# Time mix's preparation with two k units among the low-rank products, and r's mixture on ScalarE and GpSimd

## The chip, the cores and the metric

The kernel runs on one core of a Trainium2 chip. The metric is the device time of one launch in microseconds, the median of several runs; before the change it is 2626.39 us in 3 runs (2619.64 to 2627.75).

## What is computed

The program is a whole two-part network on 272 rows (16 meta rows and 256 inputs) of 1024 features: a first part with attention, a gated layer, a *time mix* and a layer of 8 experts, and a second part of two blocks. The change lies in the time mix alone. Cut to what matters here:

```python
dx_prev, dx_next = shift(x, 1) - x, shift(x, -1) - x
xs = x[None] + mu[0] * dx_prev + mu[1] * dx_next          # six mixtures
r, k, v = xs[0] @ w_r, xs[1] @ w_k, xs[2] @ w_v
lw[n] = tanh(xs[3] @ w1[n]) @ w2[n]                       # n: the two directions
decay = exp(-exp(-softplus(-(w0 + lw)) - 0.5))
a[n]  = sigmoid(a0 + (xs[4] @ a1[n]) @ a2[n])
g  = sigmoid(xs[5] @ g1) @ g2
kk = k * k_k;  kk = kk / max(norm_by_head(kk), 1e-12)
kd[n] = k * (1 + (a[n] - 1) * k_a)
y = scan(r, decay[0], kd[0], v, kk, a[0]) + reverse_scan(r, decay[1], kd[1], v, kk, a[1])
```

Behind it stand a norm by head, a bonus, the gate g, the output product and a layer norm.

## The kernel before, in words

Every engine has a program of its own, written out by hand: TensorE (PE), VectorE (DVE), ScalarE (ACT), GpSimd (POOL) and SyncE (SP). Each engine runs its instructions strictly in that order, and they meet through counting semaphores: `pe.at("k_sq", f)` is the point at which ACT has finished the square of tile f. Nothing is planned at run time, so an instruction that waits holds up all that stands behind it on its engine.

Activations lie with 128 features on partitions and the 272 rows along the free axis, so a tensor is 8 tiles of 128x272, called f or k = 0..7. A *unit* is one output tile: 8 matmuls of 128x272 that sum over k (`unsplit_units`, L358; the trace shows each of these float32 matmuls as two records, so x16 for a unit).

The time mix runs, on PE: eight units of v (L358), the first halves of the two low-rank chains (`lora_in`, L1015), their second halves (`lora_out`, L1026, 32 products), eight units of k (L358) with, two units behind each, a head sum of the squares of kk (L1044), the gate's hidden layer in 128 and in 32 columns (L1054), the spread of the reciprocal norm over the heads (L999, 8 tiles of two products), and eight units of r (L358), into which the first products of the scan are set: `first` (L1079) behind r 3 and the transposes `forward` (L1091) behind r 5. Then comes the scan over ten groups (5 chunks in 2 directions), in three waves of 4, 4 and 2 groups (`pre` L1148/L1157, `back` L1102/L1112, levels L1120, `res` L1171/L1172, `upd` L1181, `y` L1194 to L1196, `grown` L1206/L1207).

Beside it DVE makes the mixtures: `mix(i, k)` is two instructions (L1413, L1415) with a wait between, in the order i = 2 (v), 3, 4 (low rank), 1 (k), 5 (gate), 0 (r), eight tiles each. Then it scans the decays (L1438) and subtracts (L1440), scales k (L1444), makes the rate (L1462) and half of k's tensors (`half_k(d, f)` L1451/L1453, four tiles at a time), takes the norm (L1466), its reciprocal (L1468), clears buffers (L1470 to L1477), multiplies kk with the spread norm (L1481), makes BE and KE (L1484, L1486), and the solves of the waves (L1503 to L1531). ACT copies finished units out of PSUM (L1270), applies the low-rank nonlinearities (L1276, L1282, 32 sigmoids), the exponentials (L1288 to L1292), the squares for the head sums (L1299), k's factor (L1310), the square root of the norm (L1313) and the gate's sigmoid (L1316). POOL does nothing in the time mix until the bonus.

PSUM has eight banks, and every user takes one by a counter that turns unless it names a bank itself; it waits for whoever held that bank before:

```python
def bank(event, *key, b=None):
    if b is None:
        b = turn[0] % 8
        turn[0] += 1
    before, holder[b] = holder.get(b), (event, *key)
```

`forward` and `back` always take banks 4 to 7 by name. So who waits for whom in the scan hangs on how often the counter was turned before it. In the kernel before, r 0 gets bank 7, r 6 bank 1 (held by r 2), `upd` 0 bank 5 and `y` 0 bank 7, both last held by the second wave's `forward`.

Of the kernel before, what the change touches and what calls it, by code (L numbers as in the profile page):

```python
# [9 lines left out]
ACT = mybir.ActivationFunctionType  # L10
# [4 lines left out]
KC = 8  # L15
# [5 lines left out]
CH = 55  # L21
# [22 lines left out]
for _n, _w in PARAMS:  # L44
# [20 lines left out]
    "rw_out": "rv k r decays exp prep rate_taken k_part less_ka bonus bonus.kd",  # L65
# [100 lines left out]
def build(nc, A, out, known=None, stages=99):  # L166
# [774 lines left out]
    def by_chunk(x):  # L941
        return x[:, :, 0:NCH * CH].rearrange("p f (c t) -> p f c t", t=CH)
# [49 lines left out]
    def rwkv_pe(pe):  # L992
# [25 lines left out]
        def lora_out(key, x):  # L1018
# [3 lines left out]
            for f in range(KC):  # L1022
                for n in range(2):
                    b, before = bank("lora", key, f, n)
                    pe.wait_ge(pe.at(*before))
                    t = e.matmul(PS[:, b, 0:T], w2v[64 * n:64 * n + 64, f * 128:(f + 1) * 128], x[64 * n:64 * n + 64, :],  # L1026
                                 start=True, stop=True)
                    t.then_inc(*pe.sig("lora_mm", key, f, n))
            pe.also("direct", "A", m)
# [19 lines left out]
        for j, w in enumerate([128, 32]):  # L1049
            b, before = bank("gate_h", j)  # L1050
            pe.wait_ge(pe.at(*before))
            for k in range(KC):
                pe.wait_ge(pe.at("mixed", 5, k))
                t = e.matmul(PS[0:w, b, 0:T], gv[:, k, j * 128:j * 128 + w], MIXED[5][:, k, :], start=k == 0, stop=k == KC - 1)  # L1054
            t.then_inc(*pe.sig("gate_h_mm", j))
        pe.also("direct", "A", m)
        pe.wait_ge(pe.at("k_norm_r"))
        for f in range(KC):
            b, before = bank("k_spread", f)
            pe.wait_ge(pe.at(*before))  # L1060
            spread(b, f).then_inc(*pe.sig("k_spread_mm", f))
# [203 lines left out]
    def rwkv_act(act):  # L1265
# [19 lines left out]
        def exps(d):  # L1285
# [3 lines left out]
            e.activation(fac[d], by_chunk(rw_s[d])[:, :, :, CH - 1], ACT.Exp, scale=-KAPPA).then_inc(*act.own())  # L1289
            act.wait_ge(act.last)  # L1290
            e.activation(KE[d], KE[d], ACT.Exp, scale=sign).then_inc(*act.sig("exp", d, "ke"))
            e.activation(RE[d], RE[d], ACT.Exp, scale=sign).then_inc(*act.sig("exp", d, "re"))  # L1292

# [10 lines left out]
        for d in range(2):  # L1304
            exps(d)
            for f in range(4 * d, 4 * d + 4):
                k_square(f)
            act.wait_ge(act.at("rate_taken", d))
            for f in range(KC):
                e.activation(rw_a[d][:, f, 0:T], rw_a[d][:, f, 0:T], ACT.Identity, bias=less_ka[:, f:f + 1],  # L1310
                             scale=par("k_a", f)).then_inc(*act.sig("k_part", d, f))
# [96 lines left out]
    def rwkv_dve(dve):  # L1408
# [8 lines left out]
        for k in range(0, KC, 2):  # L1417
# [4 lines left out]
            e.tensor_copy(rw_e[:, r, T:T + 1], H[:, r, T - 1:T]).then_inc(*dve.own())  # L1422
# [6 lines left out]
        for i in (3, 4, 1, 5, 0):  # L1429
            for k in range(KC):  # L1430
                mix(i, k)

        def decays(d):
            dve.wait_ge(dve.at("lora", "w_lora", 7, 1))
            dve.wait_ge(dve.at("c_rw"))
            dve.wait_ge(dve.last)
            for f in range(KC):
                e.tensor_tensor_scan(rw_s[d][:, f, :], cst[:, 0:TS], rw_c[d][:, f, :], 0.0, MUL, ADD).then_inc(*dve.own())  # L1438
            dve.wait_ge(dve.last)
            e.tensor_tensor(rw_c[d], rw_s[d], rw_c[d], SUB).then_inc(*dve.sig("decays", d))  # L1440

# [45 lines left out]
        for d in range(2):  # L1487
            half_k(d, 4)
# [1856 lines left out]
```

## Time and profile before

| | |
|---|---|
| median of 3 runs | 2626.39 us (2619.64 to 2627.75) |
| profiled execution, its own time | 2621.39 us |
| its span | 2619.5 us |
| mean granted clock of TensorE | 0.981 |
| time mix, up to the scan | about 406 to 530 us |
| scan | about 530 to 750 us |

The profile is a page of one execution (busy time of every engine, the share of it in 40 slices, the chain of waits, the costliest groups), and behind it the trace, which answers by instruction: a timeline of one engine in a stretch, its waits by releaser, the busy time of all engines in a stretch. In a timeline row the first number is the start from the beginning of the span, the second the busy time of the group, then the engine, line, operation, output and inputs, the count, and in brackets how long the engine was idle before and what released it.

### The profile page before, as it was taken

Reading aid. Unit: us, or ns where it says so; the run is one execution under the profiler, and the core shown is the slowest. Engines: PE = TensorE matmul, PEld = TensorE weight load, DVE = VectorE, ACT = ScalarE, POOL = GpSimd, SP = SyncE. Lnnn points to the kernel's source line nnn. Section 1 sums busy time; section 2 is a strip of 40 time slices with the busy share of each in tenths; the row PEclk is TensorE's granted clock in tenths of the full one; section 3 lists DMA queues with packets and bytes.
Section 4 is the critical chain, followed back from the end, with each engine's and each line's share of the span. In section 5 each row is a group of like instructions: output and inputs, shape, how many; then the busy total and the mean of one; then the engine's idle time right before and its main releaser. Section 6 shows DMA issues by size and latency. Waiting matters only on the chain. (4 is left out here: it accounts for less than half of the span.)

```text
span 2619.5 us, 47732 instructions
## 1 busy us (share of the span) xinstructions
PE 2518.9 (96%) x20277; PEld 2083.1 (80%) x20277; DVE 1974.1 (75%) x2831; ACT 1531.2 (58%) x2229; POOL 176.8 (7%) x192
## 2 busy tenths in 40 slices
PE   8999999999998999999999999999999999999998
PEld 7779997688976667676676767666897999998998
DVE  7855538654446999898999999988686885677874
ACT  5634423522223778787887878786546664537653
POOL 0000000020002260000000000010010201010201
PEclk9989999999999999999999999999999999999999
DMA  7325543230032899999999999997454645444742
GB/s 203 105 65 162 177 161 87 91 103 4 4 112 82 322 383 370 377 373 377 371 370 379 369 374 375 375 367 297 122 165 128 193 153 172 148 138 145 207 137 97
DMA packets 264613, 565.86 MB, mean 216 GB/s; under 512 B 25996, under 2 KB 204356, under 8 KB 221260
## 3 DMA queue, kind: packets, MB, share of 16 engines
q1 hardware_dynamic: 257580, 547.02, 59.5%
q0 software_dynamic: 5248, 10.23, 1.3%
q10 hardware_dynamic: 1568, 5.51, 0.6%
q8 instruction: 162, 2.65, 0.4%
q14 instruction: 55, 0.45, 0.0%
HBM read 545.41 MB, written 11.53 MB: 213 GB/s over the span
## 5 line engine op out<-in xcount | busy, mean ns | idle before, releaser
L319 DVE TENSOR_TENSOR wl<-raw,wh 128x1024 fp32r<-128x1024 f32 (+1 forms) x610 | 741.6, 1223 | 264.4 <-ACT wh L310 248.5
L310 ACT ACTIVATE wh<-raw 128x1024 fp32r<-128x1024 f32 (+1 forms) x610 | 640.5, 1054 | 415.6 <-PE PS L163 400.7
L319 DVE TENSOR_TENSOR wl<-early,wh 128x1024 fp32r<-128x1024 f32 x384 | 469.5, 1238 | 53.2 <-ACT wh L310 35.4
L310 ACT ACTIVATE wh<-early 128x1024 fp32r<-128x1024 f32 x384 | 405.3, 1060 | 126.0 <-PE PS L163 113.8
L161 PE MATMUL PS<-wh,xe_h 128*96 128x512 f32 x896 | 357.4, 399 | 9.3 <-DVE xe_l L2095 5.6
L162 PE MATMUL PS<-wl,xe_h 128*96 128x512 f32 x896 | 353.7, 395 | 0.0
L163 PE MATMUL PS<-wh,xe_l 128*96 128x512 f32 x896 | 353.7, 395 | 0.0
L161 PE MATMUL PS<-b_hn_h,wh 128*128 128x256 f32 (+1 forms) x1152 | 331.6, 288 | 1.4 <-DVE b_t L2890 0.8
L162 PE MATMUL PS<-b_hn_l,wh 128*128 128x256 f32 (+1 forms) x1152 | 325.7, 283 | 0.0
L163 PE MATMUL PS<-b_hn_h,wl 128*128 128x256 f32 (+1 forms) x1152 | 325.6, 283 | 0.0
L161 PEld LDWEIGHTS PS<-b_hn_h,wh 128*128 128x128 f32 (+1 forms) x1152 | 219.1, 190 | 5.7 <-issue 2.6
L162 PEld LDWEIGHTS PS<-b_hn_l,wh 128*128 128x128 f32 (+1 forms) x1152 | 219.1, 190 | 0.7
L163 PEld LDWEIGHTS PS<-b_hn_h,wl 128*128 128x128 f32 (+1 forms) x1152 | 219.1, 190 | 0.3
L161 PEld LDWEIGHTS PS<-wh,xe_h 128*96 128x96 f32 x896 | 145.2, 162 | 73.6 <-DVE xe_l L2095 6.0
L163 PEld LDWEIGHTS PS<-wh,xe_l 128*96 128x96 f32 x896 | 145.1, 162 | 63.4
L162 PEld LDWEIGHTS PS<-wl,xe_h 128*96 128x96 f32 x896 | 145.4, 162 | 59.0
L161 PE MATMUL PS<-wh,mh_h 128*96 128x512 f32 x448 | 177.4, 396 | 0.0
L163 PE MATMUL PS<-wh,mh_l 128*96 128x512 f32 x448 | 176.9, 395 | 0.0
L162 PE MATMUL PS<-wl,mh_h 128*96 128x512 f32 x448 | 175.8, 392 | 0.0
L161 PE MATMUL PS<-ff_x_h,wh 128*128 128x272 f32 x352 | 102.1, 290 | 0.5 <-DVE ff_x_l L495 0.3
L163 PE MATMUL PS<-ff_x_h,wl 128*128 128x272 f32 x352 | 101.8, 289 | 0.0
L162 PE MATMUL PS<-ff_x_l,wh 128*128 128x272 f32 x352 | 101.3, 288 | 0.0
(495 smaller groups left out, 4903.2 us busy)
## 6 DMA issues: line engine op xcount, KB each, us to landing
early<-in_moe_in SPq DMA_DIRECT2D x128, 1024.0 KB, 7.0
raw<-in_moe_in SPq DMA_DIRECT2D x96, 1024.0 KB, 7.0
raw<-in_w_in SPq DMA_DIRECT2D x76, 1024.0 KB, 5.6
early<-in_moe_out SPq DMA_DIRECT2D x64, 1024.0 KB, 7.4
raw<-in_moe_out SPq DMA_DIRECT2D x48, 1024.0 KB, 6.7
raw<-in_attn_w_in SPq DMA_DIRECT2D x24, 512.0 KB, 5.6
raw<-in_rw_w_rkv SPq DMA_DIRECT2D x12, 1024.0 KB, 5.2
raw<-in_ffn_w_gate SPq DMA_DIRECT2D x11, 1024.0 KB, 5.4
```

Of the source, the lines that this page charges most:

```text
L161: e.matmul(o, wh, xh, start=start, stop=False)
L162: e.matmul(o, wh, xl, start=False, stop=False)
L163: return e.matmul(o, wl, xh, start=False, stop=stop)
L310: act.e.activation(st.two(n)[0], st.raw(n), ACT.Copy).then_inc(*act.sig("hi", st.name, n, sem=f"hi_{st.name}"))
L319: dve.e.tensor_tensor(lo, st.raw(n), hi.bitcast(F32), SUB).then_inc(*dve.sig("lo", st.name, n, sem=f"lo_{st.name}"))
```

## The change

On PE the second halves of the low-rank chains take banks 4 to 7 by name, and k's units take banks 0 to 3 by name; k 0 stands in the middle of the first chain's 16 products and k 1 in the middle of the second's. The head sums stand four units behind (0 to 3 behind k 4 to k 7), the last four between the gate's 128 and 32 columns. The head sum takes bank 4, the gate 5 and 6, the spread 0, 1, 2, 3, 7 and again 0, 1, 2. All these no longer turn the counter.

On DVE the sixteen instructions of r's mixture (i = 0) are gone. ACT, as its first work in the time mix, makes 16 scaled copies (mu times the shifted difference), and POOL 16 instructions of two inputs of 128x272 that combine them with H. From tile 4 on ACT's second copy waits until POOL has finished tile k-4.

ACT's exponentials KE and RE of direction 1 move behind the square root. DVE takes k's tiles between a decay's scans and its subtraction; the clearing of `sc_pad` moves between the norm and its reciprocal; `half_k(1, 0)` and `half_k(1, 4)` move behind the reciprocal and ahead of the products with the spread, and `half_k(0, 4)` moves ahead of the norm (both second halves stood behind BE and KE).

```diff
-    "rw_out": "rv k r decays exp prep rate_taken k_part less_ka bonus bonus.kd",
+    "rw_out": "shifted scaled rv k r decays exp fac prep rate_taken k_part less_ka bonus bonus.kd",
-    def unsplit_units(pe, st, event, units, X, Tn, x_event=None):
+    def unsplit_units(pe, st, event, units, X, Tn, x_event=None, at=None):
...
-            b, before = bank(event, i)
+            b, before = bank(event, i, b=at)
...
+        def lora_out(key, x, f):
...
+            for n in range(2):
+                b, before = bank("lora", key, f, n, b=4 + (2 * f + n) % 4)
...
+        def k_unit(u):
+            unsplit_units(pe, SA, "k", [u], MIXED[1], T, ("mixed", 1), at=u % 4)
...
-        lora_out("w_lora", rw_l)
-        lora_out("a_lora", rw_l2)
-        for u in range(KC + 2):
-            if u == 2:
-                b, before = bank("k_norm")
-                pe.wait_ge(pe.at(*before))
-            if u < KC:
-                unsplit_units(pe, SA, "k", [u], MIXED[1], T, ("mixed", 1))
-            if u >= 2:
-                f = u - 2
-                pe.wait_ge(pe.at("k_sq", f))
-                e.matmul(PS[0:16, b, 0:T], by_head[:, f, :], rw_q[:, f % 4, :], start=f == 0, stop=f == KC - 1).then_inc(
-                    *pe.sig("k_norm_mm", f))
+        for x, (key, y) in enumerate((("w_lora", rw_l), ("a_lora", rw_l2))):
+            for f in range(KC):
+                lora_out(key, y, f)
+                if f == 3:
+                    k_unit(x)
+        k_bank, before = bank("k_norm", b=4)
+        pe.wait_ge(pe.at(*before))
...
+        for u in range(2, KC):
+            k_unit(u)
+            if u >= 4:
+                head_sum(u - 4)
...
-            b, before = bank("gate_h", j)
+            b, before = bank("gate_h", j, b=5 + j)
...
+            if j == 0:
+                for f in range(4, KC):
+                    head_sum(f)
...
-            b, before = bank("k_spread", f)
+            b, before = bank("k_spread", f, b=(0, 1, 2, 3, 7)[f % 5])
...
+        for k in range(KC):
+            act.wait_ge(act.at("shifted", k // 2 * 2))
+            e.activation(MIXED[0][:, k, :], rw_e[:, k, 1:T + 1], ACT.Copy, scale=par("mu", 48 + k)).then_inc(
+                *act.sig("scaled", k, 0))
+            if k >= 4:
+                act.wait_ge(act.at("mixed", 0, k - 4))
+            e.activation(rw_q[:, k % 4, :], rw_e[:, k, 0:T], ACT.Copy, scale=par("mu", k)).then_inc(*act.sig("scaled", k, 1))
...
+        act.wait_ge(act.at("mixed", 0, KC - 1))
+        k_square(0)
+        k_square(1)
+        rate_exps(0)
+        exps(0)
+        k_square(2)
+        k_square(3)
+        rate_exps(1)
+        k_part(0)
+        for f in range(4, KC):
+            k_square(f)
+        k_part(1)
         act.wait_ge(act.at("k_norm"))
         e.activation(n16, n16, ACT.Sqrt).then_inc(*act.sig("k_norm_root"))
+        exps(1)
...
-        for i in (3, 4, 1, 5, 0):
+        for i in (3, 4, 1, 5):
...
+            for f in (2 * d, 2 * d + 1):
+                kk(f)
+            dve.wait_ge(done)
             e.tensor_tensor(rw_c[d], rw_s[d], rw_c[d], SUB).then_inc(*dve.sig("decays", d))
...
         decays(0)
         decays(1)
...
+        rate(0)
+        kk(4)
+        kk(5)
+        rate(1)
+        half_k(0, 0)
+        kk(6)
+        kk(7)
+        half_k(0, 4)
         dve.wait_ge(dve.at("k_norm_mm", KC - 1))
         e.tensor_scalar(n16, ps("k_norm", p=16), 1e-24, None, MAX).then_inc(*dve.sig("k_norm"))
+        e.memset(PAD, 0.0).then_inc(*dve.own())
         dve.wait_ge(dve.at("k_norm_root"))
         e.reciprocal(r16, n16).then_inc(*dve.sig("k_norm_r"))
-        for x in (PAD, XC):
-            e.memset(x, 0.0).then_inc(*dve.own())
+        half_k(1, 0)
+        half_k(1, 4)
+        e.memset(XC, 0.0).then_inc(*dve.own())
...
-        for d in range(2):
-            half_k(d, 4)
...
+        for k in range(KC):
+            pool.wait_ge(pool.at("scaled", k, 0))
+            e.tensor_tensor(MIXED[0][:, k, :], H[:, k, :], MIXED[0][:, k, :], SUB).then_inc(*pool.own())
+            pool.wait_ge(pool.at("scaled", k, 1))
+            pool.wait_ge(pool.last)
+            e.tensor_tensor(MIXED[0][:, k, :], MIXED[0][:, k, :], rw_q[:, k % 4, :], ADD).then_inc(*pool.sig("mixed", 0, k))
```

PE's order around the low-rank products, before (`raw` is the weight, `mix` the mixture, `rw_l` the low-rank hidden layers, `rw_q` the squares; L358 x8 is one unit):

```order
L1015 MATMUL PS<-mix_136,raw_54 128x272 x8
L1026 MATMUL PS<-rw_l,raw_53 128x272 x16
L1026 MATMUL PS<-rw_l_140,raw_54 128x272 x16
L358 MATMUL PS<-mix_139,raw_55 128x272 x16
L358 MATMUL PS<-mix_139,raw_53 128x272 x8
L1044 MATMUL PS<-rw_q,CB 16x272
```

and after the change:

```order
L1015 MATMUL PS<-mix_136,raw_54 128x272 x8
L1025 MATMUL PS<-rw_l,raw_53 128x272 x8
L358 MATMUL PS<-mix_139,raw_55 128x272 x8
L1025 MATMUL PS<-rw_l,raw_53 128x272 x8
L1025 MATMUL PS<-rw_l_140,raw_54 128x272 x8
L358 MATMUL PS<-mix_139,raw_55 128x272 x8
L1025 MATMUL PS<-rw_l_140,raw_54 128x272 x8
L358 MATMUL PS<-mix_139,raw_53 128x272 x16
```

Two units of k moved from behind the 32 low-rank products into them, and the first head sum no longer stands behind the third unit.

PE's order from the last units of k to the spread, before:

```order
L358 MATMUL PS<-mix_139,raw_55 128x272 x8
L1044 MATMUL PS<-rw_q,CB 16x272 x3
L1054 MATMUL PS<-mix_137,raw_53 128x272 x8
L1054 MATMUL PS<-mix_137,raw_53 32x272 x8
L999 MATMUL PS<-r_125,CB 64x272 x16
```

and after the change:

```order
L358 MATMUL PS<-mix_139,raw_55 128x272 x8
L1046 MATMUL PS<-rw_q,CB 16x272
L1061 MATMUL PS<-mix_137,raw_53 128x272 x8
L1046 MATMUL PS<-rw_q,CB 16x272 x4
L1061 MATMUL PS<-mix_137,raw_53 32x272 x8
L999 MATMUL PS<-r_125,CB 64x272 x16
```

The last four head sums moved behind the gate's first product, and only its second, of 32 columns, lies between them and the spread.

DVE's order around the reciprocal norm `r_125`, before (`rw_111` is kk, `rw_113` and `rw_120` belong to direction 1's half of k):

```order
L1466 TENSOR_SCALAR n_124<-PS 16x272
L1468 RECIPROCAL r_125<-n_124 16x272
L1470 MEMSET sc_pad 128x1792
L1470 MEMSET sc_xc 128x392
L1471 MEMSET rw_sm_129 128x512
L1472 MEMSET rw_sm_130 128x512
L1477 MEMSET sc_xc 128x14 x2
L1481 TENSOR_TENSOR rw_111<-rw_111,PS 128x272 x8
```

and after the change:

```order
L1504 TENSOR_SCALAR n_124<-PS 16x272
L1505 MEMSET sc_pad 128x1792
L1507 RECIPROCAL r_125<-n_124 16x272
L1489 TENSOR_TENSOR rw_113<-rw_113,rw_109 128x1104
L1491 TENSOR_TENSOR rw_120<-rw_120,rw_113 128x1104
L1489 TENSOR_TENSOR rw_113<-rw_113,rw_109 128x1104
L1491 TENSOR_TENSOR rw_120<-rw_120,rw_113 128x1104
L1510 MEMSET sc_xc 128x392
L1511 MEMSET rw_sm_129 128x512
L1512 MEMSET rw_sm_130 128x512
L1517 MEMSET sc_xc 128x14 x2
L1521 TENSOR_TENSOR rw_111<-rw_111,PS 128x272 x8
```

Four instructions of 128x1104 now stand between the reciprocal and the products of kk with the spread norm in PSUM, and the clearing of `sc_pad` stands ahead of the reciprocal.

## Rows read from the trace of the kernel before

**Rows 1.** The page's first part: busy time, share, count by engine
```profile
PE 2518.9 (96%) x20277; PEld 2083.1 (80%) x20277; DVE 1974.1 (75%) x2831; ACT 1531.2 (58%) x2229; POOL 176.8 (7%) x192
```
**Rows 2.** PE timeline, 395 to 560: start, us, line, tiles, count, [idle before <-releaser]
```profile
408.37 31.94 PE L358 MATMUL PS<-mix,raw 128*128 128x272 f32 x125 [3.96 <-DVE mix L1415]
...
448.26 2.10 PE L1026 MATMUL PS<-rw_l,raw 64*128 64x272 f32 x16
...
450.61 9.41 PE L1026 MATMUL PS<-rw_l,raw 64*128 64x272 f32 x48 [0.25 <-ACT rw L1282]
...
503.95 3.85 PE L1054 MATMUL PS<-mix,raw 128*32 128x272 f32 x16 [2.59 <-DVE n L1466]
...
507.74 5.22 PE L999 MATMUL PS<-r,CB 16*64 16x272 f32 x32
...
512.89 16.93 PE L358 MATMUL PS<-mix,raw 128*128 128x272 f32 x64
...
542.25 7.50 PE L358 MATMUL PS<-mix,raw 128*128 128x272 f32 x32
```
**Rows 3.** PE's groups of instructions by line, 405 to 540; idle before, releaser
```profile
L1044 PE MATMUL PS<-rw_q,CB 128*16 128x272 f32 x16 | 4.9, 397 | 2.4 <-ACT rw_q L1299 2.4
```
**Rows 4.** ACT timeline, 395 to 560
```profile
424.99 1.77 ACT L1270 ACTIVATE rw<-PS 128x272 f32<-128x272 f32 x4 [18.07 <-PE PS L358]
...
450.07 12.20 ACT L1282 ACTIVATE rw<-PS,PAR 128x272 f32<-128x272 f32 x32
...
486.40 2.04 ACT L1291 ACTIVATE rw<-rw 128x2208 f32<-128x2208 f32 x1
...
502.63 1.28 ACT L1313 ACT_TABLE_LOAD   x1
```
**Rows 5.** DVE timeline, 395 to 560
```profile
417.09 0.50 DVE L1415 SCALAR_TENSOR_TENSOR mix<-rw_e,PAR,mix 128x272 f32<-128x272 f32 x1
...
455.45 0.50 DVE L1415 SCALAR_TENSOR_TENSOR mix<-rw_e,PAR,mix 128x272 f32<-128x272 f32 x1
...
504.39 1.84 DVE L1468 RECIPROCAL r<-n 16x272 f32<-16x272 f32 x1 [0.49 <-ACT n L1313]
...
506.55 1.55 DVE L1470 MEMSET sc_pad<- 128x1792 f32 x1 [0.32 <-issue]
...
509.12 0.48 DVE L1472 MEMSET rw_sm<- 128x512 f32 x1
...
522.95 1.30 DVE L1451 TENSOR_TENSOR rw<-rw,rw 128x1104 f32<-128x1104 f32 x1
...
544.43 0.63 DVE L1514 SCALAR_TENSOR_TENSOR sc_lb<-PS,c_rw,sc_lb 128x392 f32<-128x392 f32 x1
```
**Rows 6.** Stretches: PE, PEld, DVE, ACT, POOL busy, PEclk, DMA share, GB/s
```profile
408.00:412.00 4.00, 3.63 (x8) 2.85 (x9) 3.86 (x11) 0.00 (x0) 0.00 (x0) 0.50 0.33 95
...
512.00:516.00 4.00, 4.00 (x13) 2.49 (x10) 3.41 (x4) 0.00 (x0) 0.00 (x0) 0.50 0.05 17
```
**Rows 7.** PE's waits in the scan, 530 to 760: total, times, longest
```profile
PE PS L1181 <- DVE sc_lb L1514: 2.7, 1, 2.7
...
PE PS L1148 <- DVE rw L1495: 1.6, 1, 1.6
...
PE PS L1091 <- ACT rw_ru L1359: 0.7, 1, 0.7
```
**Rows 8.** DVE timeline, 800 to 822, the residuals behind the output product
```profile
812.52 0.44 DVE L520 SCALAR_TENSOR_TENSOR H<-H,PS 128x272 f32<-128x272 f32 x1 [2.56 <-PE PS L163]
```
**Rows 9.** POOL timeline, two stretches far behind the time mix
```profile
931.55 4.94 POOL L2458 TENSOR_TENSOR sin<-sin,cos 128x256 f32<-128x256 f32 x1
...
2201.47 0.74 POOL L3121 TENSOR_TENSOR b_k_r<-b_m,b_q_r 128x256 fp32r<-128x256 f32 x1
```
**Rows 10.** DVE timeline beside POOL's instruction at 2201.47
```profile
2187.41 1.22 DVE L319 TENSOR_TENSOR wl<-raw,wh 128x1024 fp32r<-128x1024 f32 x1 [1.14 <-ACT wh L310]
...
2201.60 1.68 DVE L319 TENSOR_TENSOR wl<-raw,wh 128x1024 fp32r<-128x1024 f32 x1 [0.91 <-ACT wh L310]
```

More of the change, by code:

```diff
@@ L1016, in lora_in @@
             t.then_inc(*pe.sig("lora_mm", key))
-        def lora_out(key, x):
+        def lora_out(key, x, f):
             m = SA.of[key]
@@ L1021, in lora_out, with head_sum @@
             pe.wait_ge(pe.at("lora_h", key))
-            for f in range(KC):
-                for n in range(2):
-                    b, before = bank("lora", key, f, n)
-                    pe.wait_ge(pe.at(*before))
[L1026 to L1029, printed above, removed]
+            for n in range(2):
+                b, before = bank("lora", key, f, n, b=4 + (2 * f + n) % 4)
+                pe.wait_ge(pe.at(*before))
+                t = e.matmul(PS[:, b, 0:T], w2v[64 * n:64 * n + 64, f * 128:(f + 1) * 128], x[64 * n:64 * n + 64, :],
+                             start=True, stop=True)
+                t.then_inc(*pe.sig("lora_mm", key, f, n))
+            if f == KC - 1:
+                pe.also("direct", "A", m)
+        def k_unit(u):
+            unsplit_units(pe, SA, "k", [u], MIXED[1], T, ("mixed", 1), at=u % 4)
         lora_in("w_lora", 3)
         lora_in("a_lora", 4)
-        lora_out("w_lora", rw_l)
-        lora_out("a_lora", rw_l2)
-        for u in range(KC + 2):
-            if u == 2:
-                b, before = bank("k_norm")
-                pe.wait_ge(pe.at(*before))
-            if u < KC:
-                unsplit_units(pe, SA, "k", [u], MIXED[1], T, ("mixed", 1))
-            if u >= 2:
-                f = u - 2
-                pe.wait_ge(pe.at("k_sq", f))
-                e.matmul(PS[0:16, b, 0:T], by_head[:, f, :], rw_q[:, f % 4, :], start=f == 0, stop=f == KC - 1).then_inc(
-                    *pe.sig("k_norm_mm", f))
+        for x, (key, y) in enumerate((("w_lora", rw_l), ("a_lora", rw_l2))):
[4 more added lines that the diff above has]
+        k_bank, before = bank("k_norm", b=4)
+        pe.wait_ge(pe.at(*before))
+        def head_sum(f):
+            pe.wait_ge(pe.at("k_sq", f))
+            e.matmul(PS[0:16, k_bank, 0:T], by_head[:, f, :], rw_q[:, f % 4, :], start=f == 0, stop=f == KC - 1).then_inc(
+                *pe.sig("k_norm_mm", f))
+        for u in range(2, KC):
+            k_unit(u)
+            if u >= 4:
+                head_sum(u - 4)
         m = SA.of["g1"]
@@ L1288, in exps, with k_part @@
             e.activation(KA[d], (rw_s if d == 0 else rw_c)[d], ACT.Exp, scale=-sign).then_inc(*act.sig("exp", d, "ka"))
-            e.activation(fac[d], by_chunk(rw_s[d])[:, :, :, CH - 1], ACT.Exp, scale=-KAPPA).then_inc(*act.own())
-            act.wait_ge(act.last)
+            e.activation(fac[d], by_chunk(rw_s[d])[:, :, :, CH - 1], ACT.Exp, scale=-KAPPA).then_inc(*act.sig("fac", d))
+        def exps(d):
+            sign = -KAPPA if d == 0 else KAPPA
+            act.wait_ge(act.at("fac", d))
             e.activation(KE[d], KE[d], ACT.Exp, scale=sign).then_inc(*act.sig("exp", d, "ke"))
             e.activation(RE[d], RE[d], ACT.Exp, scale=sign).then_inc(*act.sig("exp", d, "re"))
+        def k_part(d):
+            act.wait_ge(act.at("rate_taken", d))
+            for f in range(KC):
+                e.activation(rw_a[d][:, f, 0:T], rw_a[d][:, f, 0:T], ACT.Identity, bias=less_ka[:, f:f + 1],
+                             scale=par("k_a", f)).then_inc(*act.sig("k_part", d, f))
         def k_square(f):
@@ L1303, in rwkv_act @@
         act.wait_ge(act.at("less_ka"))
-        for d in range(2):
[L1305 to L1311, printed above, removed]
+        act.wait_ge(act.at("mixed", 0, KC - 1))
[10 more added lines that the diff above has]
+        k_part(1)
         act.wait_ge(act.at("k_norm"))
         e.activation(n16, n16, ACT.Sqrt).then_inc(*act.sig("k_norm_root"))
+        exps(1)
         for j, w in enumerate([128, 32]):
@@ L1421, in rwkv_dve @@
             e.tensor_scalar(rw_e[:, r, 0:1], H[:, r, 0:1], -1.0, None, MUL)
-            e.tensor_copy(rw_e[:, r, T:T + 1], H[:, r, T - 1:T]).then_inc(*dve.own())
+            e.tensor_copy(rw_e[:, r, T:T + 1], H[:, r, T - 1:T]).then_inc(*dve.sig("shifted", k))
             dve.wait_ge(dve.last)
@@ L1433, in decays, with rate @@
         def decays(d):
-            dve.wait_ge(dve.at("lora", "w_lora", 7, 1))
             dve.wait_ge(dve.at("c_rw"))
-            dve.wait_ge(dve.last)
             for f in range(KC):
+                dve.wait_ge(dve.at("lora", "w_lora", f, d))
                 e.tensor_tensor_scan(rw_s[d][:, f, :], cst[:, 0:TS], rw_c[d][:, f, :], 0.0, MUL, ADD).then_inc(*dve.own())
-            dve.wait_ge(dve.last)
+            done = dve.last
+            for f in (2 * d, 2 * d + 1):
+                kk(f)
+            dve.wait_ge(done)
             e.tensor_tensor(rw_c[d], rw_s[d], rw_c[d], SUB).then_inc(*dve.sig("decays", d))
+        def rate(d):
+            dve.wait_ge(dve.at("lora", "a_lora", 7, 1))
+            dve.wait_ge(dve.at("exp", d, "ka"))
+            e.tensor_tensor(BE[d], KA[d], rw_a[d], MUL).then_inc(*dve.sig("rate_taken", d))
         def kk(f):
@@ L1486, in rwkv_dve @@
             e.tensor_tensor(KE[d], KE[d], rw_kk, MUL).then_inc(*dve.sig("prep", d, "ke"))
-        for d in range(2):
-            half_k(d, 4)
         def received(f, n):
```

10 lines of the change are left out of this document (1 added, 9 removed).

## The prediction

> **What bounds the kernel now.** I read the page's totals first: PE is busy for 2518.9 of 2619.5 us [rows 1], so only what shortens PE's waits, or adds to them, moves the end. The change touches the time mix alone, so I next read PE's timeline from 395 to 560 and looked for brackets. The reader is to see four small holes before the scan: 3.96 us ahead of v's units, 0.25 in the low-rank products, 2.59 ahead of the gate's 32 columns [rows 2], and 2.4 in all ahead of head sums [rows 3]. The low-rank stretch has no large bracket, yet is slow: the first 16 records take 2.10 us, the next 48 take 9.41 [rows 2], because ACT's 32 sigmoids take 12.20, or 0.381 each [rows 4]. In the scan PE's waits are 2.7 us at `upd`, 1.6 at `pre` and 0.7 at `forward` [rows 7]. So the change cannot win much more than ten microseconds, and it is measured against 2626: 0.3% is 7.9 us, about what a measurement of this kernel can tell from no change.
>
> The sum is made against the profiled execution, 2621.4 us (span 2619.5 and 1.9 around it), which lies 5.0 under the median of the runs.
>
> **Head sums.** They now stand four units behind the unit that they need, and the last four behind the gate's 128 columns. The waits for the squares, 2.4 us in three places [rows 3], go: **-2.4**. Of the squares only the last is late enough to matter, and it has a gate product of 3.7 us before it.
>
> **The norm.** The wait of 2.59 ahead of the gate's 32 columns came from a bank that the norm (L1466) had to free [rows 2]. The gate now has a bank of its own, and the norm runs beside it. What is late next is the reciprocal: behind the last head sum come the norm (about 0.4), ACT's table load of 1.28 and the root [rows 4], beside them the clearing of `sc_pad` of 1.55, then the reciprocal of 1.84 [rows 5]: 0.4 + 1.7 + 1.84, some 4.0 us, against PE's gate product of 3.85 less its tail. PE waits about 0.3: **-2.3** (bounds -2.6 and -1.5).
>
> **k among the low-rank products.** A unit costs PE 7.50 / 2 = 3.75 us [rows 2], and two move into the stretch where ACT is the slow one. Were they hidden as far as PE's own work allows, the stretch would take 32 products at 2.10 / 8, or 8.4 at most and 7.5 at the pitch without the tail, and two units of 3.66, 14.7 us together; it takes 11.7 and 7.3 now, 19.0. That is -4.4. But the products now have four banks, so ACT has only four results, 1.5 us, to work on while PE is in a unit, and then stands idle for 3.66 - 1.5 = 2.1, twice. ACT's 12.2 become 16.4 behind its start at 450.07 [rows 4], which is 466.5 against 467.3: **-1.0** (bounds -4.4 and 0). I take the end near 0, since the count of banks gives it.
>
> So the spread starts 5.7 earlier, at about 502.0 where it started at 507.74 [rows 2].
>
> **The spread.** Before, it took 5.15 us and DVE followed [rows 2]. Now its sixth tile needs bank 0, which DVE's first product with the spread frees, and ahead of that product stand four instructions of `half_k` at 1.30 [rows 5], 5.1 at their pitch, and three clearings that end 1.5 us after `sc_pad`'s (start 506.55 and 1.55, the last at 509.12 and 0.48) [rows 5]. The reciprocal lets both engines go at once. PE writes five tiles in 3.3 us and stops; DVE's first product ends 5.1 + 1.5 + 0.5 behind, and three tiles at 0.65 follow: 9.1 us in place of 5.15: **+4.0**. The four instructions are saved behind BE and KE, where nobody waited for them: the first scan products only need BE and KE, which come no later.
>
> **The clock.** After the idle 3.96 us the granted clock was 0.50, the lower level of 1.2 GHz, from 408 to 412, and again 0.50 from 512 to 516, some microseconds behind the hole of 2.59 [rows 6]. In the second, four units of r took 16.93 instead of 4 x 3.66 = 14.6 [rows 2], a loss of 2.3. Now PE stops for about 4 us in the spread, so I expect the lower level again at r's first units: **0** (bounds -2.3, should the stretch not come, and +1.1, should r lie wholly in the 6.8 us of it).
>
> **The scan's banks.** 51 turns of the counter (32 + 8 + 1 + 2 + 8) become named banks, so everything behind gets a bank three lower. r 0 moves from bank 7 to 4 and r 6 from 1 to 6. Bank 6 was last written by `forward` 0, so r 6 waits for DVE's four instructions that read it, the last from 544.43 on for 0.63 [rows 5]; r 6 started at 542.25 [rows 2]. That is a new wait of 2.8 in which r 7, `first` 4 to 7 and all of the scan stand behind r 6; the 1.6 at `pre` [rows 7] is paid out of it: +1.2. `back` 0 now takes a bank that ACT empties last, +0.9. `upd` 0 and `forward` 1 no longer wait (2.7 and 0.7 [rows 7]), but `y` 0 now takes the bank of `forward` 1 just behind them, which the same DVE instructions free; `upd` itself, 3 us, is what is gained: -2.5. In the second wave `y` 2 waits so too, +3.0 by the first wave's size, and the small ones at `back` and `forward` cancel to within 0.1: **+2.7** in all. The trace has no row for the new waits; the nearest are those of [rows 7], which bound the term from -3.4 (both waits go and none comes) to +6.
>
> **Behind the scan** the layer norm's first sum gets the bank of the last residual, where it had that of the third. The residual is 0.44 [rows 8] and as much again to be told of: **+0.8**.
>
> **r's mixture.** DVE loses 16 instructions, 7.6 us at their pitch, and its last one would end at 448.3 in place of 455.9 [rows 5]; no PE work waits for DVE there, as the scans need ACT's sigmoids. ACT's 16 copies, 6.4 us at 0.4, lie in the 18.07 that it is idle ahead of v's first copies [rows 4]. ACT's extra table load and moved KE and RE (2.04 each [rows 4]) end some 4 us before the gate's bank is wanted by r 1. POOL's 16 instructions are new work; the nearest row is 0.74 [rows 9], 12 us in all, with until r's units to do it. What they can cost is DVE: a subtraction of 1.22 alone took 1.68 when it began under POOL's 0.74 [rows 10], so about 0.46 for each that collides. Before v's last tile, ready at 417.6 [rows 5], up to 12 can collide, 5.5 us. PE needs that tile at about 423.0 (ACT's row at 424.99 [rows 4], less four matmuls), so 5.4 are free, since PE runs its first products at half clock: **+0.3** (bounds 0 and +3.5, with 0.74 for each). The Trainium skill, "SBUF — State Buffer", section "Who interferes with whom", speaks against this part: a VectorE instruction with two SBUF inputs and a GpSimd instruction that reads SBUF exclude each other, and whoever comes second waits for the whole of the other. By it the sum would have the end +3.5 in place of +0.3.
>
> Together: -2.4 - 2.3 - 1.0 + 4.0 + 0 + 2.7 + 0.8 + 0.3 = **+2.1**, that is 2623.5 against the profiled execution and 2628.5 against the median. The three runs spread over 8 us, so I take the middle, **2626.0**: no change that can be told.
>
> **Rivals.**
> - *The preparation's gain stays* (chance 0.13). The products hide k (-4.4), the scan's old waits go without new ones (-3.4), the clock does not fall (-2.3), and POOL collides with nothing: the sum becomes 2.1 - 3.4 - 6.1 - 2.3 - 0.3 = -10.0, 2616. For it: each of the holes is there in the rows. Against it: the four banks and DVE's order behind the reciprocal.
> - *GpSimd is starved, and with it ScalarE* (0.11, slower). A POOL instruction that takes 0.74 alone took 4.94 under a closed row of DVE subtractions [rows 9]. If DVE's mixtures keep POOL out until they end at 448.3, ACT's copy for tile 4 waits for POOL's tile 0, and v's copies out of PSUM stand behind it on ACT; the low-rank hidden layer wants the bank of v 0 at 440.8. PE then waits for 8 us if only POOL's last tile is outstanding, and for 14.7 if all four are; +11 gives 2637. It decides from the point where tile 3 of r's mixture is later than 440. Against it: DVE was the one that gave way at 2201.60 [rows 10], and `mix` waits between its two instructions.
> - *The lock costs its full price* (0.14). DVE loses 0.74 with each of 12 instructions, 8.9 us against 5.4 free, +3.5 in place of +0.3: 2629, within no change.
> - My sum: 0.62.
>
> **How the numbers follow.** Faster by over 7.9 is the first rival; slower by over 7.9 the second, with 0.01 to 0.02 from the upper bounds of scan and lock together; the rest is no change: 0.13, 0.74, 0.13. The range runs from the first rival, 2616, to just short of the second, 2635; my sum's bounds, about -8 and +9, lie in it.
>
> **What would show it.** Right: the spread starts near 502 and stops for 4 us behind its fifth tile, while DVE does `half_k`; ACT is idle twice in the low-rank products; r 6 waits near 2.8, no wait at `upd` 0, one of 3 at `y` 2; PE's scan ends within 3 us of before. Wrong: a start of the low-rank chain behind 441 (starvation), v's units with new holes (the lock), the spread without a stop, or r at full clock.

## The result and the profile after

| | before | after |
|---|---|---|
| median | 2622.73 us (7 runs) | 2632.98 us (7 runs) |
| ratio | 1 | 1.0028, 95% interval 1.0018 to 1.0039 |
| span of the profiled execution | 2619.5 us | 2628.2 us |
| mean granted clock | 0.981 | 0.982 |

By the ratio over the runs the change made the kernel slower by 0.28%, 7.3 us (4.7 to 10.2 by its interval; the two medians lie 10.25 apart): inside the range, but not the "no change" that was forecast, and clear of the measurement. One execution of e1 below, 8253.71 us where its eleven others took 2627 to 2639, is in no ratio.

The ledger below sets the start of the same instruction on PE in both timelines against each other. Each line shows how much later (+) the changed kernel was at that place, and how much of it came since the line before.

| place on PE | before, us | after, us | later by | since |
|---|---|---|---|---|
| low-rank products start | 448.26 | 448.55 | +0.3 | +0.3 |
| k 2 starts (before: 459.95 and two units of 3.66) | 467.27 | 469.61 | +2.3 | +2.0 |
| spread starts | 507.74 | 504.63 | -3.1 | -5.4 |
| r 0 starts | 512.89 | 514.60 | +1.7 | +4.8 |
| `first` 0 starts | 529.74 | 532.29 | +2.6 | +0.8 |
| `forward` 0 starts | 540.63 | 543.91 | +3.3 | +0.7 |
| r 6 starts | 542.25 | 548.68 | +6.4 | +3.1 |
| `pre` 0 starts | 554.80 | 559.53 | +4.7 | -1.7 |
| last `y` of the scan | 745.89 | 752.98 | +7.1 | +2.4 |
| layer norm behind it | 812.32 | 819.99 | +7.7 | +0.6 |

From there to the end of the program the distance lies between 5.3 and 8.7 us.

The waits that the change was to remove are gone. Head sums have no idle time left, where it was 2.4 [rows 3] (PE's groups by line):

```profile
L1046 PE MATMUL PS<-rw_q,CB 128*16 128x272 f32 x16 | 4.5, 396 | 0.0
```

PE's timeline through the low-rank stretch, which answers to the rows at 448.26 and 450.61 [rows 2]: the products (L1025) come in three pieces with k 0 and k 1 (L358 x16) between, and k 2 starts at 469.61.

```profile
448.55 1.19 PE L1025 MATMUL PS<-rw_l,raw 64*128 64x272 f32 x8
450.90 1.86 PE L1025 MATMUL PS<-rw_l,raw 64*128 64x272 f32 x8 [1.17 <-ACT rw L1299]
452.69 3.93 PE L358 MATMUL PS<-mix,raw 128*128 128x272 f32 x16
456.55 6.18 PE L1025 MATMUL PS<-rw_l,raw 64*128 64x272 f32 x32
462.66 3.93 PE L358 MATMUL PS<-mix,raw 128*128 128x272 f32 x16
466.52 3.16 PE L1025 MATMUL PS<-rw_l,raw 64*128 64x272 f32 x16
469.61 11.27 PE L358 MATMUL PS<-mix,raw 128*128 128x272 f32 x48
```

On ACT's timeline the reader is to see two idle stretches of 3.82 us among the 32 sigmoids, where they were one row of 12.20 [rows 4]:

```profile
450.36 3.13 ACT L1299 ACTIVATE rw<-PS,PAR 128x272 f32<-128x272 f32 x8
457.31 3.13 ACT L1299 ACTIVATE rw<-PS,PAR 128x272 f32<-128x272 f32 x8 [3.82 <-PE PS L1025]
...
467.29 3.13 ACT L1299 ACTIVATE rw<-PS,PAR 128x272 f32<-128x272 f32 x8 [3.82 <-PE PS L1025]
```

Then PE through the spread: a wait of 0.44 for the reciprocal, five tiles (x20), a stop of 4.26 us for DVE's first product L1521, three tiles, r.

```profile
504.63 2.81 PE L999 MATMUL PS<-r,CB 16*64 16x272 f32 x20 [0.44 <-DVE r L1507]
511.69 2.98 PE L999 MATMUL PS<-r,CB 16*64 16x272 f32 x12 [4.26 <-DVE rw L1521]
514.60 17.76 PE L358 MATMUL PS<-mix,raw 128*128 128x272 f32 x64
```

DVE beside it: the reciprocal, then the four instructions of `half_k` (the first and the last are shown), clearings, and the first product at 511.21, 6.6 us behind the end of the reciprocal.

```profile
502.79 1.78 DVE L1507 RECIPROCAL r<-n 16x272 f32<-16x272 f32 x1
504.50 1.23 DVE L1489 TENSOR_TENSOR rw<-rw,rw 128x1104 f32<-128x1104 f32 x1
...
508.33 1.31 DVE L1491 TENSOR_TENSOR rw<-rw,rw 128x1104 f32<-128x1104 f32 x1
...
511.21 0.42 DVE L1521 TENSOR_TENSOR rw<-rw,PS 128x272 f32<-128x272 f32 x1
```

PE ahead of r 6, and PE's waits from 530 to 770 (total, times, longest). The waits of 2.7 at `upd` and of 1.6 at `pre` [rows 7] are not among them; in their place stand 2.8 before r 6 (L358), 3.6 before `y` (L1204, 2.7 of it `y` 2) and 0.6 before `forward` 0 (L1101).

```profile
548.68 7.57 PE L358 MATMUL PS<-mix,raw 128*128 128x272 f32 x32 [2.79 <-DVE sc_lb L1552]
```

```profile
...
PE PS L1204 <- DVE sc_lb L1552: 3.6, 2, 2.7
...
PE PS L1101 <- ACT rw L1280: 0.6, 1, 0.6
```

Stretches of the changed kernel (busy time of PE, PEld, DVE, ACT, POOL, then the granted clock): 0.61 and 1.00 at v's first units, and the lower level, 0.50, from 508 to 520, in the stop and behind it, where the kernel before had 0.50 from 512 to 516 [rows 6].

```profile
408.00:412.00 4.00, 3.71 (x10) 2.93 (x11) 3.93 (x7) 0.94 (x4) 3.51 (x4) 0.61 0.28 91
412.00:416.00 4.00, 4.00 (x19) 3.30 (x19) 3.93 (x6) 1.69 (x4) 3.18 (x4) 1.00 0.02 4
508.00:512.00 4.00, 0.31 (x2) 0.29 (x4) 3.74 (x10) 0.70 (x3) 0.00 (x0) 0.50 0.14 47
512.00:516.00 4.00, 4.00 (x15) 2.09 (x12) 3.06 (x7) 0.00 (x0) 0.00 (x0) 0.50 0.00 0
516.00:520.00 4.00, 4.00 (x10) 2.96 (x10) 4.00 (x3) 0.00 (x0) 0.00 (x0) 0.50 0.00 0
```

Last, POOL beside DVE. POOL's two instructions of r's first tile, and DVE's instructions at the same time: a `mix` instruction takes 0.50 alone [rows 5] and 1.00 beside POOL, and a multiplication of one input of two elements (L1452) 0.72, where it takes 0.16 alone. DVE finishes v's last tile at 424.5 where it had it at 417.6 [rows 5]. PE waits for v's tiles twice, 0.59 and 0.89 us, and its units of v end 0.3 us later.

```profile
407.71 1.06 POOL L1668 TENSOR_TENSOR mix<-H,mix 128x272 f32<-128x272 f32 x1 [406.78 <-ACT mix L1284]
408.92 0.76 POOL L1671 TENSOR_TENSOR mix<-mix,rw_q 128x272 f32<-128x272 f32 x1
```

```profile
408.06 1.00 DVE L1444 SCALAR_TENSOR_TENSOR mix<-rw_e,PAR,H 128x272 f32<-128x272 f32 x1
...
411.10 0.72 DVE L1452 TENSOR_SCALAR rw_e<-H 128x2 f32<-128x2 f32 x1
...
423.58 0.88 DVE L1446 SCALAR_TENSOR_TENSOR mix<-rw_e,PAR,mix 128x272 f32<-128x272 f32 x1
```

### The profile page after: what moved, and what is told of

The parts are those of the page before. It is cut to its first block and busy times, and to the rows that moved or that the text cites. A ratio compares the mean times of both kernels' runs of the same rounds, so it can differ in the third digit from the quotient of the medians.

```text
span 2628.2 us, 47762 instructions
## 1 busy us (share of the span) xinstructions
PE 2518.6 (96%) x20277; PEld 2082.2 (79%) x20277; DVE 1973.6 (75%) x2815; ACT 1539.1 (59%) x2246; POOL 191.9 (7%) x208
## 5 line engine op out<-in xcount | busy, mean ns | idle before, releaser
L358 PE MATMUL PS<-mix,raw 128*128 128x272 f32 x384 | 95.4, 409 | 8.2 <-DVE mix L1446 5.4
```

## The experiments

Theory A: the time is a sum of small waits in separate places, namely banks in the low-rank stretch, DVE's order at the spread, and the rotated banks of the scan; r's mixture is free. The rivals say that what is saved ahead of the scan is given back later, or that GpSimd beside VectorE is the cost. Ratios are against the kernel before, with 95% intervals; the changed kernel stands at 1.0028.

| run | edit | ratio | interval |
|---|---|---|---|
| e1 | after, k 0 and k 1 behind the products | 1.0035 | 1.0022 to 1.0048 |
| e2 | after, old banks in the scan | 1.0013 | 1.0001 to 1.0026 |
| e3 | after, `half_k(1, .)` late | 1.0013 | 1.0003 to 1.0023 |
| e4 | after, r's mixture on DVE | 1.0024 | 1.0011 to 1.0038 |
| e5 | after, k strewn among the products | 1.0037 | 1.0024 to 1.0049 |
| e6 | before, new banks in the scan | 1.0021 | 1.0011 to 1.0031 |
| e7 | e2 + e3 + e5 | 0.9987 | 0.9975 to 0.9999 |
| e8 | e7, r's mixture on DVE | 0.9980 | 0.9968 to 0.9992 |
| e9 | e2 + e3 + e4 + e10 | 0.9970 | 0.9957 to 0.9983 |
| e10 | after, eight banks, k behind the products | 1.0023 | 1.0010 to 1.0036 |
| e11 | before, r's mixture moved | 0.9994 | 0.9980 to 1.0008 |
| e12 | e9, other banks for two `upd` and two `y` | 0.9958 | 0.9939 to 0.9977 |

### The low-rank stretch: e1, e5, e10

```diff
+        for x in range(2):
+            k_unit(x)
```

(e1: behind the loop over the products, and `if f == 3: k_unit(x)` taken out.)

> The changed kernel with k 0 and k 1 put behind the 32 low-rank products again; banks stay as changed (four for the products). Theory A (the four banks tie TensorE to ScalarE's pace, and the unit in the middle only adds an idle stretch that the four banks cannot bridge): products are paced by ScalarE to about 462.4, two units follow, k 2 starts at 469.8 where the changed kernel has 469.6: no gain, within 1 us of the changed kernel, about +7.5 us (1.0028) against before. Theory B (the place of the k units is the fault by itself): k 2 starts near 467.5 as before the change, 2 us faster than the changed kernel, about 1.0020.

PE's timeline of e1, then of e10, which differs in the banks alone:

```diff
-                b, before = bank("lora", key, f, n, b=4 + (2 * f + n) % 4)
+                b, before = bank("lora", key, f, n, b=(4 + 2 * f + n) % 8)
...
-            unsplit_units(pe, SA, "k", [u], MIXED[1], T, ("mixed", 1), at=u % 4)
+            unsplit_units(pe, SA, "k", [u], MIXED[1], T, ("mixed", 1), at=(4 + u) % 8)
```

> The changed kernel with that one edit alone: low-rank products in eight banks, k's units behind them. Theory A: the stretch takes 19.0 us in place of 21.1, the spread starts 2 us earlier, about +5.4 us against before (1.0021). Rival: the stretch stays at 20.5 us, under 1 us of gain, 1.0026.

```profile
448.21 1.19 PE L1025 MATMUL PS<-rw_l,raw 64*128 64x272 f32 x8
450.57 10.92 PE L1025 MATMUL PS<-rw_l,raw 64*128 64x272 f32 x56 [1.17 <-ACT rw L1299]
461.42 18.60 PE L358 MATMUL PS<-mix,raw 128*128 128x272 f32 x80
```

```profile
448.65 2.10 PE L1025 MATMUL PS<-rw_l,raw 64*128 64x272 f32 x16
451.00 9.43 PE L1025 MATMUL PS<-rw_l,raw 64*128 64x272 f32 x48 [0.26 <-ACT rw L1299]
460.36 18.60 PE L358 MATMUL PS<-mix,raw 128*128 128x272 f32 x80
```

From the first product to the first unit of k it is 13.2 us with four banks (448.21 to 461.42) and 11.7 with eight (448.65 to 460.36), as before the change. With the two units, k 2 comes 20.5, 19.0 and, in the changed kernel, 21.06 us behind the first product. So 1.5 of the 2.0 us lost are the four banks, and 0.5 the units' place. e1's 20.5 lie nearer to theory A (469.8, or 21.2 behind the first product at 448.55) than to theory B (467.5, or 19.0). ACT's 32 sigmoids, of e1 and then of e10, are one row without a hole in both, as before the change:

```profile
450.03 12.19 ACT L1299 ACTIVATE rw<-PS,PAR 128x272 f32<-128x272 f32 x32
```

```profile
450.46 12.22 ACT L1299 ACTIVATE rw<-PS,PAR 128x272 f32<-128x272 f32 x32
```

So ACT sets the pace, and what differs is the work that PE leaves behind when it goes on to k: ACT works on for 0.80 us in e1 (461.42 to 462.22), and for 2.32 in e10 (460.36 to 462.68) and in the kernel before (459.95 to 462.27 [rows 4]). The difference, four sigmoids for four banks, is the 1.5. The kernel before thus already hid 2.3 of the 7.3 us of k's two units. The times alone do not tell the three kernels apart: e1 lies 1.8 us above the changed kernel and e10 1.3 below it, and the intervals overlap. Two units in the middle with eight banks were not run.

e5 sets one matmul of k behind every second product:

```diff
-                if f == 3:
-                    k_unit(x)
+                t = e.matmul(PS[:, kb, 0:T], cols_view(256)(SA.slot(m))[:, k, u % 2 * 128:u % 2 * 128 + 128],
+                             MIXED[1][:, k, :], start=k == 0, stop=k == KC - 1)
...
```

> The changed kernel with the 16 matmuls of k 0 and k 1 strewn among the 32 low-rank products, one behind every second product, where the change has them as two blocks of eight. Theory A (ScalarE's idle stretches of 3.8 us, twice, are what the blocks cost): ScalarE is never idle for over 1 us, TensorE bounds the stretch with 32 x 0.25 + 16 x 0.46 = 15.4 us, k 2 starts at about 464.5 in place of 469.6, 4 to 5.5 us faster than the changed kernel, about +2.5 us (1.0010) against before. Rival (the four banks are the limit however the units lie): k 2 at 468 or later, under 2 us of gain.

```profile
449.62 0.73 PE L1025 MATMUL PS<-rw_l,raw 64*128 64x272 f32 x4
450.28 0.72 PE L1047 MATMUL PS<-mix,raw 128*128 128x272 f32 x2
...
470.67 11.16 PE L358 MATMUL PS<-mix,raw 128*128 128x272 f32 x48
```

A miss for theory A. The stretch takes 21.05 us (449.62 to 470.67), and PE has no hole in it: two products and one matmul of k come at a pitch of 21.05 / 16 = 1.32 us (0.66 from the products' start to k's), where 2.10 / 8 = 0.26 for a product and 3.66 / 8 = 0.46 for a matmul of k in a unit of its own would make 0.98. The alternation costs PE 0.3 us per round, 16 times; whether the shapes, the weight loads or the waits between them do it, no run tells. It is not ACT, which is idle for 0.45 us in each round. The rival's time came, 21 us, but not by its reason, the banks. The estimate of 15.4 us was worked out from unmixed rows and does not hold for mixed ones.

### The spread: e3

```diff
-        half_k(1, 0)
-        half_k(1, 4)
         e.memset(XC, 0.0).then_inc(*dve.own())
...
             e.tensor_tensor(KE[d], KE[d], rw_kk, MUL).then_inc(*dve.sig("prep", d, "ke"))
+        half_k(1, 0)
+        half_k(1, 4)
```

> The changed kernel with half_k(1, 0) and half_k(1, 4) behind BE and KE again. Theory A: the stop of 4.3 us in the spread goes almost whole (the clearings of 1.5 us still stand ahead, hidden by five tiles), r starts 4 to 5 us earlier, and with the shorter hole the clock's low stretch costs no more than before: 4 to 5.5 us faster than the changed kernel, about +2.5 us (1.0010) against before. Rival (VectorE's four instructions only move to where they are waited for, at the scan's pre, which wants direction 1's half): half of it is given back, about +5 us (1.0020).

```profile
505.06 5.48 PE L999 MATMUL PS<-r,CB 16*64 16x272 f32 x32 [0.44 <-DVE r L1507]
510.47 16.66 PE L358 MATMUL PS<-mix,raw 128*128 128x272 f32 x64
```

The spread is one row of 32 again and r starts 5.41 us behind it, where it was 9.97: 4.6 us, as theory A has it. The ratio falls from 1.0028 to 1.0013, 3.9 us; that part of it is given back is neither shown nor excluded by the interval. The wait in which the rival had it, PE's at `pre` for DVE, is not among e3's waits in the scan.

### The scan's banks: e2, e6, e12

```diff
+        turn[0] += 3
```

(e2: ahead of r in `rwkv_pe` of the changed kernel; e6: `turn[0] += 5` at the same place of the kernel before.)

> The changed kernel with the bank counter turned three further ahead of r, so that r and the scan have the banks that they had before the change. Theory A (the shifted banks cost on their own): the wait of 2.8 before r 6 goes, the waits at pre, forward and upd of the kernel before come back, PE's place at the end of the scan is 3 to 4 us earlier than in the changed kernel: about +4 us (1.0015) against before. Rival (what the scan's banks cost is returned by waits elsewhere, and the clock is what matters): less than 1 us of difference to the changed kernel, about 1.0027.

> The kernel before with nothing but the bank counter turned five further ahead of r, which gives r and the scan the banks of the changed kernel. Theory A: the new waits (2.8 before r 6, 2.7 before y 2, 0.6 before forward 0) and those that go leave +3 to +4 us against before (1.0012 to 1.0015). Rival (the waits only show in the changed kernel because of its late spread): within 1 us of before.

PE's waits from 525 to 752 for e2, then for e6:

```profile
...
PE PS L1193 <- DVE sc_lb L1554: 2.7, 1, 2.7
...
PE PS L1160 <- DVE rw L1535: 1.5, 1, 1.5
```

```profile
...
PE PS L1196 <- DVE sc_lb L1516: 3.6, 2, 2.7
PE PS L358 <- DVE sc_lb L1516: 2.8, 1, 2.8
...
PE PS L1093 <- ACT rw L1272: 0.6, 1, 0.6
```

Each set of waits goes with its banks, whatever stands ahead: e2 has the old ones (L1193 is `upd`, L1160 is `pre`), e6, which changes nothing else of the kernel before, the new ones (L1196 is `y`, L358 r 6, L1093 `forward`). The price is 3.9 us in e2 and 5.5 in e6 (2.9 to 8.1), at and above the upper end of what was expected. Thirteen traces show the size, those of both kernels and of e1 to e11. Between the start of `first` 0 and that of the last `y`, PE waits for other engines for 14.6 us in each of the seven with the new banks, and for 10.9 to 11.2 in the six with the old ones. The stretch takes 217.7 to 223.3 us (mean 220.2) against 212.3 to 216.2 (mean 213.7). So 3.6 of 6.5 us are the waits themselves. Most of the rest is PE's busy time, 203.4 against 200.9 in the mean, but there the two groups overlap (200.7 to 206.9 and 198.7 to 203.5), and so does the granted clock (0.96 to 0.99 and 0.98 to 1.00). In e1, e3 and e5 the clock fell right behind the wait ahead of r 6, and two units of r took 9.26 us, where they take 7.57 in the other four with the new banks; e1's row:

```profile
546.41 9.26 PE L358 MATMUL PS<-mix,raw 128*128 128x272 f32 x32 [2.80 <-DVE sc_lb L1552]
```

That the waits bring the clock down elsewhere in the scan too is not shown: in the pair of traces in the ledger it is 0.98 in both, and PE is busy for 1.0 us less after the change.

e12 names the banks of the users that still waited:

```diff
-            b = take("upd", g)
+            b = take("upd", g, b=(1, 2)[g] if g < 2 else None)
+            turn[0] += g < 2
...
-            b = take("y", g)
+            b = take("y", g, b=(3, 0)[g] if g < 2 else None)
+            turn[0] += g < 2
```

> The first run of this group with upd 0 and 1 in banks 1 and 2 and y 0 and 1 in banks 3 and 0 by name, so that none of them takes a bank that the second wave's forward has just filled; all else keeps its bank. Theory A (the wait of 2.7 at upd 0 is the bank and nothing else): it goes, no new wait at y 0, 2.5 to 3 us faster than the first run, 0.9963. Rival (PE only meets VectorE's or ScalarE's work there a little later): a wait of 2 us or more at y 0 or in grown, under 1 us of gain.

PE's waits from 520 to 745:

```profile
PE PS L1124 <- ACT sc_xu L1365: 5.2, 3, 2.0
PE PS L1160 <- DVE rw L1529: 1.5, 1, 1.5
PE PS L1132 <- issue: 1.1, 4, 0.5
PE PS L1114 <- ACT rw_ru L1386: 0.8, 1, 0.8
PE PS L1103 <- ACT rw_ru L1386: 0.7, 1, 0.7
PE PS L1194 <- issue: 0.4, 1, 0.4
```

These are all that there are: the wait of 2.7 at `upd` (here L1194) is gone and none for DVE or ACT came in its place. The ratio falls from 0.9970 to 0.9958, 3 us, though the intervals overlap.

### r's mixture: e4, e11

e4 takes the copies from ACT, the sums from POOL, and puts i = 0 back in DVE's loop; e11 makes the opposite move in the kernel before.

```diff
-        for i in (3, 4, 1, 5):
+        for i in (3, 4, 1, 5, 0):
```

> The changed kernel with r's mixture on VectorE again, no ScalarE copies and no GpSimd instructions there. Theory A (the exclusive port costs VectorE as much as the 16 instructions cost it, all under cover): VectorE reaches the decays' scans within 1 us of the changed kernel, v's units have no holes, PE is 0.3 us earlier at the low-rank chain, the time within 1 us of the changed kernel, about 1.0027. Rival (the port conflicts are what makes the change slower): 3 us or more faster than the changed kernel, 1.0015 or below.

> The kernel before with nothing but r's mixture moved to ScalarE and GpSimd. Theory A (the exclusive port gives back on VectorE what the 16 instructions saved, under cover): v's last tile is 6 to 7 us later, two holes of under 1 us in v's units, VectorE starts the decays' scans within 1 us of before, the time within 1.5 us of before (0.9994 to 1.0006). Rival (the move alone makes it slower): +3 us or more, 1.0012.

PE's timeline of e11, two of v's units:

```profile
418.75 3.94 PE L358 MATMUL PS<-mix,raw 128*128 128x272 f32 x16 [0.34 <-DVE mix L1423]
423.57 18.61 PE L358 MATMUL PS<-mix,raw 128*128 128x272 f32 x80 [0.88 <-DVE mix L1423]
```

Neither time is told from its base (1.0024 against 1.0028; 0.9994 against 1). v's units have two holes as in the changed kernel, 0.34 and 0.88 (0.59 and 0.89 there). DVE began the scans of the decays at 455.80 in the changed kernel and at 456.26 before: the 7.6 us of instructions taken from it came back as time lost beside POOL.

For PE the move was not free. From the start of v's units to that of the low-rank chain it takes 32.8 us in all eight traces with the move and 31.0 to 31.1 in five of the six without. The sixth is the kernel before, with 32.5: there the granted clock was 0.68 from 412 to 416, where the changed kernel had 1.00. e4's row of v's units, which has no hole, and that stretch of the kernel before:

```profile
409.93 31.25 PE L358 MATMUL PS<-mix,raw 128*128 128x272 f32 x128 [3.96 <-DVE mix L1438]
```

```profile
412.00:416.00 4.00, 4.00 (x13) 3.07 (x13) 3.86 (x11) 0.00 (x0) 0.00 (x0) 0.68 0.01 4
```

So the 0.3 us of the ledger is chance, a slow stretch in the one trace of the kernel before, and 1.7 to 1.8 is what the move costs PE in the others. e4's theory A, with 0.3, missed that.

### All together: e7, e8, e9

> All three together on the changed kernel: k 0 and k 1 strewn among the products, the old banks in the scan, half_k of direction 1 late. Theory A (the costs are separate places and add up): 7.4 - 5 - 3.5 - 4.7 = -5.8 us against before, 0.9978, with 2 us more or less by the clock. Rival (they cover each other, so that later ones are hidden once the first is gone): no better than -2 us, 0.9992 or above.

> The same three, and r's mixture on VectorE as in the kernel before. Theory A (the split mixture neither gives nor takes): within 1 us of the run with all three. Rival (with TensorE earlier by 5 us VectorE's mixture of r comes to be waited for, at the scans of the decays): 2 us or more slower than the run with all three; or, if GpSimd's port is the cost, 1 us or more faster.

> From the fastest so far (r's mixture on VectorE, the old banks in the scan, half_k of direction 1 late), with the low-rank products in all eight banks by name and k's eight units behind them, as in the kernel before. Theory A (four banks in place of eight are what the low-rank stretch lost): from the start of the second halves to k 2 it takes 19.0 us as before the change, where four banks took 20.5 to 21.1; 1.5 to 2 us faster than the run with all four edits, about -7 us against before (0.9973). Rival (the stretch is ScalarE's 12.5 us of sigmoids in any case): 20.5 us and no gain, 0.9980.

e7 gains 10.8 us on the changed kernel where 13.2 were expected, and of those 5 were e5's, which gave nothing alone; e2 and e3 alone gave 3.9 each. So the places do not hide each other. e8 lies 1.8 us below e7, as v's units have it (31.0 against 32.8): the size of its rival on GpSimd (1 us or more faster) and not of theory A, though the intervals overlap. e9's low-rank stretch is that of the kernel before (11.7 us). It lies 2.6 us below e8, where 1.5 to 2 were expected, again with intervals that overlap, and e9, at 0.9970, is faster than both kernels. e12 is the fastest: 2609.41 us against 2619.77 in the same set of runs.

## Why the prediction was wrong

| term | forecast | in the trace after |
|---|---|---|
| head sums | -2.4 | -2.4 |
| norm | -2.3 | -2.15 (2.59 less 0.44) |
| k among the low-rank products | -1.0 | +2.0 |
| spread | +4.0 | +4.8 (9.97 against 5.15) |
| clock, in r's units | 0 | +0.8 |
| the scan's banks | +2.7 | +4.5 |
| behind the scan | +0.8 | +0.6 |
| r's mixture | +0.3 | +0.3 |

The trace's terms come to about +8.5. Between k 2 and the spread 0.9 us more went than the idle times show, which leaves +7.6, against +7.7 in the ledger. Those 0.9 are most likely changes between units and head sums, of which the changed kernel has fewer: a unit takes 3.87 us between two head sums and 3.73 in a row of three, a head sum 0.56 alone and 0.46 in a row of four.

**The step that failed** is the one on k: "ACT's 12.2 become 16.4 behind its start at 450.07, which is 466.5 against 467.3: -1.0 (bounds -4.4 and 0)". The mechanism stood in it (four results, then idle ACT), but its size was 2.1 us for each stop and the runs show 3.82. When PE goes on to k at 452.69, ACT has 0.80 us of work left and not 1.5 (its row ends at 453.49); the unit takes 3.86 and not 3.66, to 456.55; and ACT starts on the next product 0.76 us after that, which the forecast put at nothing. With 3.82 twice in place of 2.1 its own sum gives 469.9, and k 2 starts at 469.61. The step also sets ACT's end against PE's start of k 2, and its two numbers differ by 0.8, not 1.0. A bound of 0 at the upper end was wrong as well: e1 and e10 show that four banks in place of eight cost 1.5 us by themselves. With +2.0 in place of -1.0 the sum is +5.1.

**The second** is the scan's banks, +2.7. The right waits stood in the right places (2.8 before r 6, 2.7 before `y` 2, none at `upd` 0), 0.9 us short of the 3.6 that they cost. The stretch grew by 4.5 in the pair of traces, and the price was 3.9 in e2 and 5.5 in e6; of what goes beyond the waits, only the fall of the clock behind r 6's wait, in three of seven traces, is seen to follow one.

**The clock and r's mixture** were put at 0 and +0.3, and the pair of traces has +0.8 and +0.3, but neither is a price. Four units of r take 16.29 to 17.76 us in the six traces with the stop in the spread, and 16.59 to 17.49 in the eight without. The 0.3 was luck, since the other traces have 1.7 to 1.8.

**What held.** The two groups of waits that go; the stop of 4 us and its cause, DVE's four instructions, by e3; v's mixtures, late by the lock. For the lock the Trainium skill, "SBUF — State Buffer", section "Who interferes with whom", has that the port pair which VectorE and GpSimd share is an exclusive lock. The trace agrees, as DVE's instruction grew by 0.50 and POOL's by 0.3 in turn, and v's last tile came 6.9 us later, near the 8.9 of the third rival.

**The rivals.** GpSimd was not starved: POOL and DVE took turns, and the fourth tile of r's mixture was done by 417. The first rival, a gain of 10, failed at the banks. The third gave the right lock, and its sign, new holes in v's units, came; its price for PE, +3.5, was about twice what the traces show. The forecast had 0.13 on slower by over 7.9 us, and 7.3 lies just short of that, with an interval that reaches past it; what was wrong is the sum's size, by about 5 us. That the range held is luck: its upper end came from the second rival, which did not happen.

## What to carry to other kernels

Before work is moved into an engine's wait, ask what that engine leaves behind for the other: that is the cover it had already (here six sigmoids of 0.38 us with eight PSUM banks and two with four), and taking banks away for the moved work can cost more than the move brings. A counter that hands out buffers in turn couples places far apart: name a few users' banks and everything behind them waits for someone else, so write down who holds each buffer, ahead and behind, or name those at the waits too (e12). A price taken from a run of equal instructions does not hold for two kinds in alternation (e5). And a term of a microsecond cannot be read from one pair of traces: behind the same hole the clock stayed low for longer in one than in the other.

## What the runs showed of the hardware

- Alternating low-rank products (64-row weights) with matmuls of k (128-row weights) cost PE 1.32 us per round of three where the unmixed pitches sum to 0.98.
- A multiplication of one input of two elements on DVE was held for 0.56 us beside POOL (0.72 against 0.16), as the large ones of two inputs were (1.00 against 0.50).
- Around the stop of 4.26 us (to 511.69) the granted clock was at the lower level from 508 to 520; after 3.96 us of idle before v's units it was at 0.61 from 408 to 412 and at 1.00 from 412 to 416, where the kernel before had 0.50 [rows 6] and 0.68. So the same hole had different stretches at the lower level behind it in the two traces.
- A wait of 2.8 us ahead of r 6 was followed by the lower level in three of seven traces: two units of r took 9.26 us there and 7.57 in the other four.
